# Two query-weight loads of a decoder block split at partition 120

## What is computed

```python
def peer_ffn(h, w_q, sub_keys, u_tab, v_tab):
    q = (ht @ w_q).reshape(T, PEER_HEADS, 2, PEER_HALF)
    sc = jnp.einsum('thpc,hpnc->thpn', q, sub_keys).astype(jnp.float32)
    s1, i1 = lax.top_k(sc[:, :, 0], PEER_TOPK)
    s2, i2 = lax.top_k(sc[:, :, 1], PEER_TOPK)
    ...
    top_s, pos = lax.top_k(cand, PEER_TOPK)
    eid = jnp.take_along_axis(cand_id, pos, axis=-1)
    g = jax.nn.softmax(top_s, axis=-1).astype(h.dtype)

    def chunk(args):
        hc, ec, gc = args
        a = jnp.einsum('cd,chkd->chk', hc, u_tab[ec])
        w = gc * jax.nn.gelu(a)
        return jnp.einsum('chk,chkd->cd', w, v_tab[ec])
```

## Time and profile before

| | us |
|---|---|
| median of three runs | 901.4 |
| lowest and highest run | 900.94, 902.09 |
| profiled execution, device time | 902.3 |
| its span in the trace | 900.5 |
| TensorE busy | 771.4 |
| VectorE busy | 613.7 |
| ScalarE busy | 346.5 |
| GpSimd busy | 288.3 |

### The profile page before, as it was taken

The page is one execution under the profiler, slowest core; times in us unless marked ns, Lnnn a source line. Parts: engine busy times, 40 slices in busy tenths (PEclk is TensorE's granted clock), DMA queues, the critical chain, the costliest instruction groups (busy, mean ns, idle before and its releaser), DMA issues.

```text
span 900.5 us, 8445 instructions
## 1 busy us (share of the span) xinstructions
PE 771.4 (86%) x2526; PEld 415.6 (46%) x2526; DVE 613.7 (68%) x1420; ACT 346.5 (38%) x1027; POOL 288.3 (32%) x279
## 2 busy tenths in 40 slices
PE   4999999999999999999997768787777777777777
PEld 2477877667556556565652323232322233222232
DVE  6788798963587977848669788758744444444445
ACT  3458688872144342523333242322422222222222
POOL 4000000000244544453637434453443334333320
PEclk9999999999999999999999998999999999999999
DMA  9968454679399999999999999999999999999995
GB/s 374 423 263 297 164 207 191 245 313 406 118 390 422 404 423 423 413 422 422 421 420 422 421 422 421 421 422 421 422 423 421 422 421 421 421 421 423 421 421 211
DMA packets 44100, 336.70 MB, mean 374 GB/s; under 512 B 4884, under 2 KB 5012, under 8 KB 7320
## 3 DMA queue, kind: packets, MB, share of 16 engines
q0 software_dynamic: 37152, 268.45, 71.9%
q1 hardware_dynamic: 6888, 67.72, 19.1%
q10 hardware_dynamic: 16, 0.00, 0.0%
HBM read 335.11 MB, written 1.05 MB: 373 GB/s over the span
## 4 chain that ended last, share of the span: by engine, by line
PE 48%; DMA 36%; DVE 10%; ACT 3%; issue 2%; POOL 1%; SPq 0%; DVEq 0%; ACTq 0%
DMA ring<-in_peer_uv,eid 26%; PE ps_y L1624 21%; DMA rows<-in_peer_uv,eid 6%; PE bank L1594 5%; DMA extra<-in_peer_uv,eid 4%; PE bank L1560 3%; DVE ring L1018 3%; PE bank L1435 2%; PE bank L1437 2%; PE bank L1436 2%; PE bank L1575 2%; PE ps_y L1435 1%; PE ps_y L1437 1%; PE ps_y L1436 1%; PE ps_y L1399 1%
## 5 line engine op out<-in xcount | busy, mean ns | idle before, releaser
L1624 PE MATMUL ps_y<-ring,diag 128*128 128x512 f32 x572 | 271.2, 613 | 55.8 <-ACT diag L1310 55.8
L589 POOL DMA_INDIRECT ring<-in_peer_uv,eid x142 | 151.0, 1064 | 413.7 <-DVE eid L924 227.3
L1018 DVE CUSTOM_DVE_ANT_0 ring<-ring,gates 128x1024 f32<-128x1024 f32 x143 | 173.2, 1224 | 99.4 <-DMA ring<-in_peer_uv,eid 98.6
L1624 PEld LDWEIGHTS ps_y<-ring,diag 128*128 128x128 f32 x572 | 107.3, 194 | 201.8 <-issue 116.2
L1298 ACT ACTIVATE mask<-mask 128x2 f32<-128x2 f32 (+1 forms) x132 | 26.7, 202 | 358.3 <-DVE mask L1018 353.3
L1310 ACT ACTIVATE diag<-ident,mask 128x128 f32<-128x128 f32 x256 | 87.3, 386 | 0.3
L1624 PE MATMUL ps_y<-rows,diag 128*128 128x512 f32 x136 | 63.6, 611 | 9.8 <-ACT diag L1310 9.8
L1303 ACT ACTIVATE mask<-g_sb,mask 128x1 f32<-128x1 f32 x256 | 61.9, 287 | 4.3
L1018 DVE CUSTOM_DVE_ANT_0 rows<-rows,gates 128x1024 f32<-128x1024 f32 x34 | 41.4, 1227 | 31.0 <-DMA rows<-in_peer_uv,eid 30.9
L653 DVE TENSOR_TENSOR w_lo<-ring,w_hi 128x512 fp32r<-128x512 f32 x76 | 50.7, 685 | 11.6 <-PE bank L1437 10.1
L1114 ACT ACTIVATE w_hi<-ring 128x512 fp32r<-128x512 f32 x76 | 45.5, 626 | 24.6 <-PE bank L1437 24.1
(11 more groups left out here) (230 smaller groups left out, 1216.2 us busy)
## 6 DMA issues: line engine op xcount, KB each, us to landing
ring<-in_ada_t SPq DMA_DIRECT2D x11, 2048.0 KB, 9.9
ring<-in_in_t SPq DMA_DIRECT2D x10, 2048.0 KB, 10.4
ring<-in_up_t SPq DMA_DIRECT2D x2, 2048.0 KB, 8.4
ring<-in_out_t SPq DMA_DIRECT2D x2, 2048.0 KB, 13.2
ring<-in_peer_uv,eid POOLq DMA_INDIRECT x142
x_sb<-in_x SPq DMA_DIRECT2D x2, 1024.0 KB, 12.0
ring<-in_ada_t SPq DMA_DIRECT2D x2, 1024.0 KB, 21.5
kz<-in_peer_t SPq DMA_DIRECT2D x1, 2048.0 KB, 22.9
```

Source lines behind the costliest of these rows:

```text
L589: pool.indirect_dma_start(uv_row(n), None, peer_uv, bass.IndirectOffsetOnAxis(ap=eid[:, n:n + 1], axis=0)).then_inc(s_uv[name], 16)
L1018: dve.tensor_tensor_reduce(u_row(n), u_row(n), h2[:, n // P, :], 1.0, 0.0, ALU.mult, ALU.add, adot[:, at:at + 1]).then_inc(s_dot, 1)
L1624: ins = pe.matmul(ps_y[:, cut], diag[:, n % ND, :], v_row(n)[:, cut], start=first, stop=last)
```

## The change

The two runs that are loaded beside the gather are each issued as two DMAs, one for partitions 0 to 119 and one for partitions 120 to 127. By its description they then use fifteen and eight DMA engines instead of sixteen. The new table `peer_parts` says how many parts a run has, and the wait in `queries` counts 16 for each part, so that for quarter 3 it goes from 48 to 80. The bytes and their places are the same.

```diff
+
+        peer_cut = 120
+        peer_parts = [[1] * len(runs) for runs in peer_runs]
+        peer_parts[3][1:] = [2, 2]
...
             def peer_run(m, r):
                 first, last = peer_from[m][r:r + 2]
-                sp.dma_start(peer_runs[m][r], peer_t[m, :, first:last, :]).then_inc(s_peer[m], 16)
+                if peer_parts[m][r] == 1:
+                    sp.dma_start(peer_runs[m][r], peer_t[m, :, first:last, :]).then_inc(s_peer[m], 16)
+                    return
+                for some in (slice(0, peer_cut), slice(peer_cut, P)):
+                    sp.dma_start(peer_runs[m][r][some], peer_t[m, some, first:last, :]).then_inc(s_peer[m], 16)
...
             def queries(t, m):
 
-                pe.wait_ge(s_peer[m // 2], 16 * len(peer_runs[m // 2]))
+                pe.wait_ge(s_peer[m // 2], 16 * sum(peer_parts[m // 2]))
```

## The result

The changed kernel takes 907.99 us (median of six runs, 906.99 to 908.51) against 901.75 us (six runs, 900.94 to 902.70) for the kernel before. The ratio is 1.0067 with a 95% interval of 1.0057 to 1.0077: 6.2 us slower. The forecast was 900.5 us, in a range of 899.4 to 902.2. The profiled execution has a span of 906.4 us, 5.9 us more than before.

A forecast was written before the change was run, and what follows sets the result against it. TensorE was taken to set the pace first, then the gather's DMA, whose slowest engine ends the kernel. Relieving one engine of 3.09 us was to bring 0.9 us, the rest nothing: 901.4 to 900.5 us, range 899.4 to 902.2.

The forecast's parts named there:

- Step (a): kz load issued at 316.94 us: one engine relieved of 3.09 us, eight get 0.39 us more, seven are as before.
- a sum of nought: Whole change: by the rule that transfers to disjoint partitions share the same engines, splitting would bring no gain.
- Step (b): yT load issued at 242.75 us, 1.78 us on each engine: nil effect, since all engines run dry at 260 us.
- The gap at 260 us: DMA share falls from 1.03 to 0.36 at 260 to 261 us; all engines were dry and started again together.
- Step (c): SyncE's queue: two more issues of about 0.33 us cost nothing; kz landing 1 us later, with 58 us of cover.
- Step (d): End of the gather: of the relieved engine's 3.09 us, 0 to 1.6 us reaches the end; 0.9 us taken.
- The stall at 376 us: GpSimd waits 7.79 us for a query product, early engines run dry; loses 0.4 us, may take the relieved engine's gain.
- The ninth row: Rival: the latest engine is among the eight with an extra row, 0.39 us later at the end; 901.8 us, chance 0.10.
- the split isn't what it says: Rival: the 120 rows go to fewer engines, say eight with 15 rows, up to 2.7 us later; 904.1 us, chance 0.05.
- All four: The rivals: nothing moves 901.4 us (0.32), whole gain 899.6 (0.10), an extra row 901.8 (0.10), another split 904.1 (0.05).
- two things said to be signs of a wrong mechanism: A change in the time before 376 us, or a rate other than 421 GB/s between 467 and 884 us.

## Why the prediction was wrong

**Step (a), the kz load: this is the step that failed.** It took a row's price of 0.39 us over from the load of 128 rows and counted rows for each engine: one relieved, eight with one more, "seven are as before". The rows are counted rightly. But a row's price hangs on how the DMA lies on the partitions: it was 0.72 us in the changed load, and the gather's rows beside it, which the step didn't count at all, took 0.58 instead of 0.31. The missing term is the half of the rate that was lost for some 13 us, 6.3 us in all. The splits at 64 and from 32 to 95, and the two with other source rows, show that the partitions written decide, and neither the number of engines nor the rows read. That engines are in each other's way is inferred from this: the gather's rows, whose own deal didn't change, were slowed too.

The Trainium skill states what would give this (SBUF - State Buffer, "Door 1: The DMA port swizzle"): partitions 0 to 31 have the same ports as 32 to 63, and 64 to 95 the same as 96 to 127, so that of the sixteen ports 0 to 63 and 64 to 127 have eight each. By it, sixteen or fifteen engines with neighbouring blocks of four or eight rows reach eight ports at a time, and 64 rows from 32 on reach all sixteen. The runs agree with it: 222 to 228 GB/s into 0 to 63 against 415 into 32 to 95, and 251 against 426 with the source rows exchanged. That each engine gets neighbouring rows in such a DMA is an assumption, since no record here has an engine's number; with it the rule and these four rates fit. The prediction used a rule on how many engines a DMA takes, and nothing on where they write. It also had a sum of nought by a rule on two transfers to disjoint partitions; the measured sum is +6.2 us, and +5.1 for the two halves of 64.

**Step (b), the yT load:** right at the end (0.9997 with that load alone split), though the same price per row was wrong here too: the rate fell to 240 GB/s, which the step had not foreseen. The gap at 260 us covered it, as the step said, and was nearly used up. In the changed kernel it is gone altogether:

```profile
260.00:261.00 1.00, 1.00 (x4) 0.42 (x3) 0.97 (x2) 0.97 (x4) 0.69 (x2) 1.00 1.00 418
```

**Step (c), SyncE's queue:** right in what it costs, though not in its number. The last row of the kz load ended at 332.9 us, and the last update of its semaphore came at 334.0 us, 17.1 us after the second issue where 11.3 us were allowed. It is first read at 389.1 us, still 55 us later.

**Step (d), what reaches the end.** Its two halves came out differently. The stall at 376 us does take most of a gain made before it: without the kz load 1.3 of 3.09 us arrive by the median. But the relieved engine was, as far as can be seen, not the latest. In the last microseconds of the kernel after

```profile
888.00:889.00 1.00, 0.95 (x3) 0.12 (x1) 0.18 (x2) 0.72 (x3) 0.00 (x0) 1.00 0.97 397
889.00:890.00 1.00, 0.77 (x2) 0.49 (x3) 0.56 (x1) 0.18 (x1) 0.00 (x0) 1.00 0.92 377
890.00:891.00 1.00, 1.00 (x3) 0.19 (x1) 0.67 (x2) 0.26 (x2) 0.00 (x0) 1.00 0.98 401
...
895.00:896.00 1.00, 1.00 (x3) 0.19 (x1) 1.00 (x3) 0.32 (x2) 0.00 (x0) 1.00 0.12 49
896.00:897.00 1.00, 0.54 (x2) 0.30 (x2) 0.99 (x3) 0.70 (x3) 0.00 (x0) 1.00 0.11 45
897.00:898.00 1.00, 1.00 (x3) 0.38 (x2) 1.00 (x1) 0.79 (x3) 0.00 (x0) 1.00 0.07 29
898.00:899.00 1.00, 1.00 (x4) 0.46 (x3) 0.10 (x2) 0.80 (x3) 0.00 (x0) 1.00 0.05 20
```

the DMA share from 888 to 891 us is 0.96 on the mean, where it had been 1.01: about one engine of sixteen is done ahead of the others. The last two rounds, cut in halves, have rows of 4 KB, and these show how far ahead. The DMA packets from 883.7 to 886 us in the kernel after, and under them those of the kernel split at 64 from 884.5 to 886.8, both counted from the first row of 4 KB:

```profile
DMA packets 139, 0.95 MB, mean 413 GB/s; under 512 B 16, under 2 KB 16, under 8 KB 30
```

```profile
DMA packets 170, 0.92 MB, mean 401 GB/s; under 512 B 19, under 2 KB 19, under 8 KB 96
```

In the kernel after 14 rows of 4 KB (30 less 16) begin in 2.3 us, one every 0.16 us, which is the time of one such row: one engine alone has come to the last rounds. With the split at 64 it is 77 in the same time, so that many engines are there together. The kernel with only the kz load split at 120 has one engine ahead as well, by some 1.4 us (first row of 4 KB at 884.48 us). So the split at 120 puts one engine ahead of the others by 1.4 to 2.4 us, and the splits at 64 and at 32 and 96 put none. That it is the relieved one is inferred, since the records don't number the engines. At the very end the shares are 0.12 and 0.11 and then 0.07 and 0.05, again two late engines, at nearly the same distances as in the earlier trace rows and 6 us later. If it is the relieved one that is first now, it was not the latest before, and the predicted gain of 0.9 us had no ground, even at the full rate. The numbers 7 and 15 that the prediction thought of for the two late engines can't both be right either, if the relieved one is 15, as it says. Which engines the two late ones are stays open.

**The reading of the stage.** The earlier trace rows had both TensorE and the DMA full before 433 us, and the prediction said that TensorE sets the pace there. That was right for gains (without the load 1.8 of 3.1 us are lost again) and wrong for losses: the DMA had only the 0.3 to 0.4 us of the stall to spare, so of 6.3 us 6.0 came to the end.

**The rivals.** Two of them had the sign, but neither had the cause. "The ninth row" gave 901.8 us, and "the split isn't what it says" gave 904.1, from rows dealt to fewer engines at the old price. All four stood within 2.7 us of the time before, because all of them kept the rate at 421 GB/s. Of the two things said to be signs of a wrong mechanism one came, a change before 376 us; the rate between 467 and 884 us stayed at 421 GB/s.

## What to carry to other kernels

Beside a stream that fills the DMA engines, keep loads in the shape that is dealt over all of SBUF, here 128 partitions, and cut them along the free dimension if they have to be cut: for the 1280 KB here, two DMAs of 128 rows cost nothing, and two of 64 rows some 5 us, while 64 rows from partition 32 on went at 415 GB/s, nearly the full rate. Ask of a changed transfer not only how many rows each engine has but what a row will cost to it and to its neighbours. Where two resources are both full, as here before 433 us, a gain on one is largely hidden by the other and a loss is paid nearly in full.

## What the runs showed of the hardware

- The partitions that a DMA covers can set the rate of everything beside it: with the DMA share at 0.93 to 1.11 the core moved 196 to 244 GB/s instead of 422, and the gather's rounds, dealt as ever, were slowed too.
- The busy share of the DMA engines doesn't show it. The digits stayed at 9; only the GB/s fell.
- The same happens without a gather: 189 and 216 GB/s against 427 and 420 in the first quarter's load.
- It is the written partitions, not the rows read: 251 GB/s into 0 to 63, 426 into 32 to 95, with the source rows exchanged.
